# Transposed x and memory as inputs, the second weight unit in halves, and a new order of the first loads

## What is computed

```python
def hybrid_layer(x, mem, pos, g_mix, w_in, w_pa, w_pb, w_pm, w_o, g_mem, w_mkv, g_mlp, w_up, w_down):
    h = rms_norm(x, g_mix)
    z = h @ w_in                      # 1024 x 5632
    ...                               # three kinds of attention on parts of z, gates on the rest
    o_m = memory_attn(q_m * scale, rms_norm(mem, g_mem), w_mkv)
    ...
    x = x + y @ w_o
    hm = rms_norm(x, g_mlp)
    x = x + jnp.square(jax.nn.relu(hm @ w_up)) @ w_down
    return x
```

## Time and profile before

| | |
|---|---|
| median of three runs | 1577.0 us (1576.68 to 1578.81) |
| the profiled execution's own time | 1576.6 us |
| its span | 1574.8 us |
| TensorE busy | 1428.4 us, 91% of the span |
| VectorE, ScalarE, GpSimd busy | 578.9, 551.9, 673.6 us |
| share of TensorE and of DMA in the chain that ended last | 76% and 20% |
| moved by DMA | 395.40 MB, mean 251 GB/s |

### The profile page before, as it was taken

The page is one execution under the profiler, slowest core; times in us unless marked ns, Lnnn a source line. Parts: engine busy times, 40 slices in busy tenths (PEclk is TensorE's granted clock), DMA queues, the critical chain, the costliest instruction groups (busy, mean ns, idle before and its releaser), DMA issues.

```text
span 1574.8 us, 17946 instructions
## 1 busy us (share of the span) xinstructions
PE 1428.4 (91%) x7601; PEld 1015.6 (64%) x7601; DVE 578.9 (37%) x885; ACT 551.9 (35%) x709; POOL 673.6 (43%) x187
## 2 busy tenths in 40 slices
PE   8999999999999999999999999999996676666666
PEld 7877788877887778887799888978841121121111
DVE  4532423336262242334743886768510010010001
ACT  6356443433535545434343344574310000000001
POOL 5846588755784658786555775010000000000000
PEclk9999999999999999999999999999997788787788
DMA  8534457588553445659825444014999999999997
GB/s 296 188 112 157 149 173 240 182 304 315 174 182 126 146 147 183 226 181 337 320 87 183 147 145 154 14 68 142 419 407 427 427 429 427 427 428 428 428 427 292
DMA packets 115517, 395.40 MB, mean 251 GB/s; under 512 B 5719, under 2 KB 9620, under 8 KB 101996
## 3 DMA queue, kind: packets, MB, share of 16 engines
q1 hardware_dynamic: 113372, 388.70, 66.3%
q0 software_dynamic: 1520, 4.49, 0.8%
q10 hardware_dynamic: 544, 1.05, 0.2%
HBM read 393.16 MB, written 1.05 MB: 250 GB/s over the span
## 4 chain that ended last, share of the span: by engine, by line
PE 76%; DMA 20%; DVE 2%; ACT 1%; issue 1%; SPq 0%; DVEq 0%; ACTq 0%
PE psum L2284 18%; PE psum L2286 17%; PE psum L2285 17%; DMA ring<-in_w_e_down 7%; PE psum L1249 7%; DMA ring<-in_w_e_gate 6%; DMA ring<-in_w_e_up 6%; PE psum L1164 2%; PE psum L2437 1%; PE psum L2464 1%; PE psum L1025 1%; PE psum L2328 1%; PE psum L2513 1%; PE psum L824 1%; PE psum L823 1%; PE psum L825 1%
## 5 line engine op out<-in xcount | busy, mean ns | idle before, releaser
L655 POOL TENSOR_TENSOR ring_lo<-ring,ring_hi 128x2048 fp32r<-128x2048 f32 x118 | 537.9, 4565 | 230.5 <-ACT ring_hi L635 230.3
L635 ACT ACTIVATE ring_hi<-ring 128x2048 fp32r<-128x2048 f32 (+1 forms) x127 | 239.9, 1889 | 317.4 <-DMA ring<-in_w_down 108.5
L2286 PE MATMUL psum<-ring_hi,hT_hi 128*128 128x512 f32 (+2 forms) x848 | 327.7, 386 | 0.0
L2285 PE MATMUL psum<-ring_lo,hT_hi 128*128 128x512 f32 (+2 forms) x848 | 327.0, 386 | 0.0
L2284 PE MATMUL psum<-ring_hi,hT_lo 128*128 128x512 f32 (+2 forms) x816 | 323.0, 396 | 0.6 <-DVE ring_lo L2638 0.2
L1249 PE MATMUL psum<-arena 128*32 128x512 f32 x796 | 142.9, 706 | 64.2 <-DMA arena<-in_w_e_down 23.4
L1249 PE MATMUL psum<-ring,arena 128*32 128x512 f32 x720 | 132.8, 727 | 60.2 <-DMA ring<-in_w_e_gate 23.0
L2286 PEld LDWEIGHTS psum<-ring_hi,hT_hi 128*128 128x128 f32 x848 | 159.2, 188 | 32.4
L2285 PEld LDWEIGHTS psum<-ring_lo,hT_hi 128*128 128x128 f32 x848 | 159.5, 188 | 28.6
L2284 PEld LDWEIGHTS psum<-ring_hi,hT_lo 128*128 128x128 f32 x816 | 153.3, 188 | 37.6 <-issue 6.8
L1249 PEld LDWEIGHTS psum<-arena 128*32 128x32 f32 x796 | 32.2, 127 | 164.9 <-issue 73.6
(11 more groups left out here) (467 smaller groups left out, 1930.3 us busy)
## 6 DMA issues: line engine op xcount, KB each, us to landing
ring<-in_w_in SPq DMA_DIRECT2D x59, 1024.0 KB, 5.1
ring<-in_w_up SPq DMA_DIRECT2D x32, 1024.0 KB, 5.5
ring<-in_w_down SPq DMA_DIRECT2D x32, 1024.0 KB, 5.3
ring<-in_w_e_down SPq DMA_DIRECT2D x16, 2048.0 KB, 20.4
arena<-in_w_e_up SPq DMA_DIRECT2D x14, 2048.0 KB, 20.6
arena<-in_w_e_down SPq DMA_DIRECT2D x12, 2048.0 KB, 23.5
ring<-in_w_e_gate SPq DMA_DIRECT2D x12, 2048.0 KB, 22.7
arena<-in_w_e_gate SPq DMA_DIRECT2D x12, 2048.0 KB, 22.9
```

What stands on the lines that cost most here:

```text
L635: act.activation(slot_hi(u)[:, 0:c, :], slot(u)[:, 0:c, :], ACT.Copy).then_inc(hi_sb, 1)
L655: eng.tensor_tensor(slot_lo(u)[:, 0:c, :], slot(u)[:, 0:c, :], slot_hi(u)[:, 0:c, :].bitcast(F32), ALU.subtract).then_inc(done, 1)
L2285: pe.matmul(dst, hi(k0 + k), w_lo, start=False, stop=False)
L2286: last = pe.matmul(dst, hi(k0 + k), w_hi, start=False, stop=stop and k == nk - 1)
```

## The change

The host passes x and the memory transposed as well (`x_t`, `mem_t`, both 1024 x 256) and the gains of `norm_mix` as 128 x 16 (`gain_cols`).

- **x in layer 0.** ScalarE and SyncE load `x_t` in halves into the place of `xn`; `hT_hi` and `hT_lo` are made from there, chunk by chunk alternately with the pieces of unit 0. The sixteen transposes of x in layer 0 and that of the gain rows go. The plain x is loaded later: ScalarE waits for unit 2 and issues it, and squares it after the high parts of units 2 and 3.
- **Unit 1 in halves.** Its load, high part, low part and products come in two halves. VectorE makes the low part of unit 2 too.
- **Memory.** The transposes of both layers go. In layer 0 GpSimd issues the load of the memory after the low part of unit 3 (and a wait for x), that of `mem_t` after unit 4's, that of the rest of `consts` after unit 5's (and a wait for the memory). In layer 1 SyncE loads `mem_t` after unit 3. ScalarE copies `mem_t` to psum, where VectorE reads it as before. The memory's row factor is computed in layer 0 alone, with a square root of its own.
- **The rest.** `keep_busy` runs five matmuls, not four. Semaphore counts follow.

```diff
-LO_VECTOR = [(l, u) for l in range(DEPTH) for u in SPLIT if (l == 0 and u < 2) or (u >= 50 and u % 4 == 2)]
+LO_VECTOR = [(l, u) for l in range(DEPTH) for u in SPLIT if (l == 0 and u < 3) or (u >= 50 and u % 4 == 2)]
...
             sp.sem_inc(slots_free, R1)
+            sp.dma_start(cols[:, 0:16], w["gain_cols"]).then_inc(const_in, 16)
             sp.dma_start(consts[:, 0:P], w["consts"][:, 0:P]).then_inc(const_in, 16)
-            gain_rows(0, "norm_mix", const_in)
...
+                    if l == 0 and u == 1:
+                        for half in range(2):
+                            cs = slice(2 * half, 2 * half + 2)
+                            sp.dma_start(slot(1)[:, cs, :], src[:, cs, :]).then_inc(landed(1) if half else half_in, 16)
+                        sp.dma_start(xT[:, 4:8, :], x_src[:, 4:8, :]).then_inc(rest_in, 16)
+                        continue
                     load(u, src, l * UNITS1 + u + 1)
+                    if l and u == R1 - 1:
+                        sp.dma_start(memT, w["mem_t"].rearrange("(c p) t -> p c t", p=P)).then_inc(late_in, 16)
...
             pe.wait_ge(const_in, 32)
-            pe.transpose(psum[:, 7, 0:16], rows1[0:16, :], ident[0:16, 0:16]).then_inc(cols_full, 1)
-            pe.wait_ge(x_in, 16)
-            half_to_features(x, 0)
-            keep_busy(6, 4)
+            keep_busy(6, 5)
             first_unit()
-            pe.wait_ge(rest_in, 16)
-            half_to_features(x, 1)
+            second_unit()
...
-                if l == 0:
-                    pe.wait_ge(cols_sb, 2)
-                pe.wait_ge(mem_in, 32)
-                to_features(mem_tok)
...
-            x_src = w["x"].rearrange("b (t p) d -> p (b t) d", p=P)
-            act.dma_start(x[:, :, 0:UN], x_src[:, :, 0:UN]).then_inc(x_in, 16)
-            act.dma_start(x[:, :, UN:D], x_src[:, :, UN:D]).then_inc(rest_in, 16)
+            act.dma_start(xT[:, 0:4, :], w["x_t"].rearrange("(c p) t -> p c t", p=P)[:, 0:4, :]).then_inc(x_in, 16)
...
+            high_half(1, g_feat[:, 0, 0, :], 0, xT)
+            act.wait_ge(slot_in[2], 16)
+            act.dma_start(x[:, :, :], w["x"].rearrange("b (t p) d -> p (b t) d", p=P)).then_inc(x_in, 16)
...
+                if l == 0:
+                    high_parts(5, 5)
+                    act.wait_ge(mem_in, 16)
+                    for t in range(TT):
+                        act.activation(mem_sq[:, t, :], mem_tok[:, t, :], ACT.Square, accum_out=means[:, TT + t:TT + t + 1]).then_inc(sq_a, 1)
+                    high_parts(6, 6)
...
+                    act.wait_ge(rows_in, 16)
+                else:
+                    act.wait_ge(late_in, 16 * (N_LATE + l))
+                act.wait_ge(turn_lo, l * 18 + 8)
+                for half in range(2):
+                    act.activation(flat[2 + half].rearrange("p (k t) -> p k t", k=4), memT[:, 4 * half:4 * half + 4, :], ACT.Copy)\
+                       .then_inc(mem_f, 1)
+                high_parts(7 if l == 0 else 4, 14)
...
-            pool.wait_ge(rest_in, 16)
-            pool.wait_ge(slot_in[2], 16)
-            pool.dma_start(mem_tok, w["mem"].rearrange("b (t p) d -> p (b t) d", p=P)).then_inc(mem_in, 16)
-            pool.dma_start(consts[:, P:], w["consts"][:, P:]).then_inc(mem_in, 16)
...
                     split_lo(pool, l, u)
+                    if l == 0 and u == 3:
+                        pool.wait_ge(x_in, 32)
+                        pool.dma_start(mem_tok, w["mem"].rearrange("b (t p) d -> p (b t) d", p=P)).then_inc(mem_in, 16)
+                    if l == 0 and u == 4:
+                        pool.dma_start(memT, w["mem_t"].rearrange("(c p) t -> p c t", p=P)).then_inc(rows_in, 16)
+                    if l == 0 and u == 5:
+                        pool.wait_ge(mem_in, 16)
+                        pool.dma_start(consts[:, P:], w["consts"][:, P:]).then_inc(mem_in, 16)
```

More of the change, by code:

```diff
@@ L2345, in first_unit, with second_unit @@
                 last.then_inc(slots_free, 1)
+            def second_unit():
+                for half in range(2):
+                    pe.wait_ge(lo_v, UC + half + 1)
+                    for t in range(TT):
+                        last = split_product(DB[1][:, t, :], tokens(hT_hi, t), tokens(hT_lo, t), 2 * half, 1, nk=2, first=2 * half,
+                                             start=half == 0, stop=False)
+                last.then_inc(slots_free, 1)
             def late_rows():
@@ L2571, in _, with low_half @@
         def _(dve):
-            def low_half(half, gain, ready):
+            def low_half(half, gain, ready, features=None):
                 for k in range(4):
@@ L2576, in low_half @@
                         dve.wait_ge(turn_a, ready + k + 2)
-                    dve.scalar_tensor_tensor(out=hT_lo[:, 4 * half + k, :], in0=flat[2 + half][:, k * T:(k + 1) * T],
+                    src = flat[2 + half][:, k * T:(k + 1) * T] if features is None else features[:, 4 * half + k, :]
+                    dve.scalar_tensor_tensor(out=hT_lo[:, 4 * half + k, :], in0=src,
                                              scalar=gain[:, 4 * half + k:4 * half + k + 1],
@@ L2638, in low_piece @@
                 dve.tensor_tensor(slot_lo(0)[:, k, :], slot(0)[:, k, :], slot_hi(0)[:, k, :].bitcast(F32), ALU.subtract).then_inc(lo_v, 1)
-            dve.wait_ge(cols_full, 1)
-            dve.tensor_copy(cols[:, 0:16], psum[:, 7, 0:16]).then_inc(cols_sb, 1)
-            dve.wait_ge(cols_sb, 1)
-            low_piece(0)
-            low_half(0, g_feat[:, 0, 0, :], 0)
-            for k in range(1, UC):
+            dve.wait_ge(const_in, 32)
+            for k in range(UC):
+                dve.wait_ge(turn_a, k + 1)
+                dve.scalar_tensor_tensor(out=hT_lo[:, k, :], in0=xT[:, k, :], scalar=g_feat[:, 0, 0, k:k + 1],
+                                         in1=hT_hi[:, k, :].bitcast(F32), op0=ALU.mult, op1=ALU.subtract).then_inc(turn_lo, 1)
@@ L2646, in _ @@
                 low_piece(k)
-            split_lo(dve, 0, 1)
+            for half in range(2):
+                cs = slice(2 * half, 2 * half + 2)
+                dve.wait_ge(hi_sb, UC + half + 1)
+                dve.tensor_tensor(slot_lo(1)[:, cs, :], slot(1)[:, cs, :], slot_hi(1)[:, cs, :].bitcast(F32), ALU.subtract).then_inc(lo_v, 1)
             for l in range(DEPTH):
-                low_half(1, g_feat[:, 0, l, :], l * 18 + 4)
+                low_half(1, g_feat[:, 0, l, :], l * 18 + 4, None if l else xT)
@@ L2659, in _ @@
-                dve.tensor_scalar(means, means, 1.0 / D, EPS, ALU.mult, ALU.add).then_inc(r_v, 1)
-                dve.wait_ge(sq_a, l * 11 + 7)
-                dve.reciprocal(r_all, roots).then_inc(r_v, 1)
-                dve.wait_ge(r_v, l * 7 + 3)
+                    dve.wait_ge(cols_sb, 1)
+                cs = slice(0, TT)
+                dve.wait_ge(sq_a, l * 12 + 4)
+                dve.tensor_reduce(means[:, cs], sums, AX_X, ALU.add).then_inc(r_v, 1)
+                dve.wait_ge(r_v, l * 9 + 1)
@@ L2680, in _ @@
                 z_tile(1)
+                if l == 0:
+                    cm = slice(TT, 2 * TT)
+                    dve.wait_ge(sq_a, 7)
+                    dve.tensor_scalar(means[:, cm], means[:, cm], 1.0 / D, EPS, ALU.mult, ALU.add).then_inc(r_v, 1)
+                    dve.wait_ge(sq_a, 8)
+                    dve.reciprocal(r_mem, roots[:, cm]).then_inc(r_v, 1)
+                    dve.wait_ge(r_v, 6)
                 for half in range(2):
-                    dve.wait_ge(turn_full, l * 8 + 3 + half)
+                    dve.wait_ge(mem_f, 2 * l + half + 1)
                     for k in range(4):
@@ L2910, in high_piece @@
                 act.activation(slot_hi(0)[:, k, :], slot(0)[:, k, :], ACT.Copy).then_inc(hi_sb, 1)
-            high_piece(0)
-            act.wait_ge(cols_sb, 1)
-            high_half(0, g_feat[:, 0, 0, :], 1)
-            for k in range(1, UC):
+            act.wait_ge(const_in, 32)
+            act.wait_ge(x_in, 16)
+            for k in range(UC):
+                act.activation(hT_hi[:, k, :], xT[:, k, :], ACT.Copy, scale=g_feat[:, 0, 0, k:k + 1]).then_inc(turn_a, 1)
                 high_piece(k)
+            for half in range(2):
+                cs = slice(2 * half, 2 * half + 2)
+                act.wait_ge(slot_in[1] if half else half_in, 16)
+                act.activation(slot_hi(1)[:, cs, :], slot(1)[:, cs, :], ACT.Copy).then_inc(hi_sb, 1)
+            high_half(1, g_feat[:, 0, 0, :], 0, xT)
+            act.wait_ge(slot_in[2], 16)
+            act.dma_start(x[:, :, :], w["x"].rearrange("b (t p) d -> p (b t) d", p=P)).then_inc(x_in, 16)
             for l in range(DEPTH):
```

112 lines of the change are left out of this document (65 added, 47 removed).

## The result

The changed kernel takes 1588.55 us in the median of five runs (1587.6 to 1589.82), the kernel before in the same comparison 1577.32: a ratio of 1.007 with a 95% interval of 1.0059 to 1.0082. It is slower by 11 us. The forecast was 1571.4, faster; the time is outside its range, and beyond the rival that gave 1580.5.

A forecast was written before the change was run, and what follows sets the result against it. TensorE was taken to set the pace to about 1100 us, expert loads after. 1.3 + 1.2 + 1.75 + 1.75 - 0.4 = 5.6 us off 1576.6 gave 1571.0, as a median 1571.4; range 1568.8 to 1575.0.

The forecast's parts named there:

- the rival that gave 1580.5: Layer 0, plain x landing very late, at 31 us: GpSimd and ScalarE wait, kernel slower at 1580.5 us; chance 0.04.
- What bounds the kernel: TensorE sets the pace to about 1100 us, expert loads after; a microsecond saved on TensorE early is one of the total.
- Step 1: Start of the kernel: unit 0 begins at 7.55 and ends at 13.85 us, a gain of 1.3 us, ends +2.3 and -0.3.
- the rival in which it is up already: Start: the clock is already up when unit 0 starts, 0.8 us are not lost, 1570.6 us; chance 0.12.
- Step 2: Layer 0, second half of x's transposes gone and the slower matmul after it: a gain of 1.2 us.
- Step 3: Memory's transposes gone in layers 0 and 1: a gain of 1.75 us in each.
- Step 4: Layer 0, units 2 to 7 in the new order of loads: nearly every unit ready when TensorE wants it, 0.4 us lost.
- ends 0 and 3: Layer 0, units 2 to 7: the least and most us that waits under the new order were taken to cost.
- all landings at 11.3: Case behind the loss of 3 us: loads take the longest row, the memory costing 2.1 us and mem_t 2.5, not added.
- the slower rival: Layer 0, plain x lands very late and holds GpSimd and ScalarE; slower by over 0.2% from a landing at 30.7; chance 0.04.
- Unit 4 ... ready at 30.1; wanted 30.5: Layer 0: x lands at 21.1, then squares 2.5, high part 1.92, low part 4.6 us make unit 4 ready at 30.1.
- ready at L + 9.0: Layer 0: if x lands at L, unit 4 is ready at L + 9.0 and TensorE waits L + 9.0 - 30.5.

The follow-up runs named there:

- e8: e5 with the loads of memory, mem_t and tables issued by SyncE and the tables' transposes behind unit 2; 1576.2 us, against 1578.4 before the change.
- e5: The changed kernel with half_r made by ScalarE, silu_c moved before the MLP and the memory's mean written to psum; 1576.66 us, against 1578.4 before the change.
- e10: e9 with the mean of x written to psum instead of SBUF in layer 0; 1574.98 us, against 1578.38 before the change.
- e9: e8 with ScalarE's unit 4 high part before x's sums, the square-root table loaded early and silu_c's tanh later; 1574.66 us, against 1578.7 before the change.
- e6: e5 with x issued at once, not behind unit 2's landing, and the tables' transposes behind unit 2; 1580.07 us, against 1578.4 before the change.

## Why the prediction was wrong, step by step

**What bounds the kernel: right.** TensorE's shift at L1039, 11.46 us (1060.15 against 1048.69), is the shift of the end, 11.2 in the medians. That they agree so closely is in part luck, as the stretch behind L1039 differs by up to 3 us between profiles.

**Step 1, the start: right, a little better.** The constants landed at 4.97 (forecast 5.4) and unit 0 began at 7.13 (7.55). The gain columns, in rows of 64 B, landed 3.1 us after issue and the constants, in rows of 512 B, 3.7, so the rule of 512 B for line rate (the Trainium skill, DMA: Bandwidth & Descriptors, the table at its head) decided nothing here. The clock did take its share, with matmuls 0.57 and 0.43 us apart, to 8.5 in this execution; the rival in which it is up already did not come about.

**Step 2, x's transposes: right.** Unit 1 ended at 18.69 (18.46 and 0.23), forecast 19.3; before, its last matmul began at 21.57.

**Step 3, the memory's transposes: right.** In layer 1 the stretch from x's second transposes to the first wait block is 486.00 - 425.23 = 60.77 us; before it was 475.02 - 412.49 = 62.53:

```profile
412.49 0.71 PE L2328 MATMUL psum<-consts,x 128*128 128x128 f32 x5
```

That is 1.76 us gained, forecast 1.75.

**Step 4, the new order: this failed,** as its term of 0.4 us lost (ends 0 and 3) came out at 17.6: the first wait block of layer 0 stands 12.7 us later, although 3.1 were gained up to the end of unit 1 and some 1.75 on the memory's transposes. Even its end of 3 was too small by its own rows: "all landings at 11.3" left out the load of x, for which the slower rival gives 4.4.
- "Unit 4 ... ready at 30.1; wanted 30.5" followed the loads, ScalarE and GpSimd, and never VectorE. TensorE needs two things for unit 4, its low part and free psum banks, and the banks wait for VectorE's row factor and z tiles. The low part was done at 34.0; the bank that unit 4 needs came free at 45.95. The step costed `half_r`, silu_c and the means at nothing without naming them. In the trace before the first two cost next to nothing (0.17 and 0.30), since they happened to fall into the 2.7 us in which GpSimd was idle; the mean had its wait already, 0.64 us.
- The unseen wait is 2.77 and 10.41 us on VectorE, 12.46 before unit 4, and 1.6 more behind it for the clock (0.50 granted from 46 to 48 us).
- The tables were costed as 0.35 us of transposes, without their landing. They stood in SyncE's queue behind unit 3 and landed at about 20.4: 1.64 us of waiting, and eight slow matmuls behind it, some 1.5 us (0.51 granted from 22 to 24 us). Unit 2's own low part, "ready at 19.3", ended at 20.28, so the tables alone are not to blame for the wait; in e8, without them, TensorE still waits 0.61 us for it. That is why unit 3 ended at 33.4 and not at 30.5.
- x landed at 24.9, not 21.1. By the forecast's own formula (ready at L + 9.0) that gives 33.9, and the low part ended at 34.0. In the changed kernel this is hidden behind VectorE's wait, in e5 and e8 it is the 2.2 us that remain. The slower rival had this mechanism and the right relation, but L was well under the 30.7 it needs; what made the kernel slower was none of the rivals.

The terms sum up: 33.38 instead of 30.5, 12.6 of waiting and 1.6 of slow clock put the first wait block of layer 0 at 91.21, 12.7 later than before. Layer 1's 1.76 make it 10.98 at 475 us. With these waits removed, the profile of e10 stands 5.45 us earlier than that of before at this place, 4.9 at L1039 and 4.2 in its own time (1572.36 against 1576.6): most of the 5.6 us forecast were there to be had in that execution, with an order of loads and of ScalarE's work that the change did not have. What the runs show is less, the 3 us of e9's ratio.

## What to carry to other kernels

Before a step is moved, ask for every small operation that it carries along what the neighbouring engine was doing when its short duration was measured; a duration of 0.17 us from a gap is no price for a place without one. Where GpSimd works nearly without pause, keep VectorE's scalings from SBUF to SBUF and its operations with two SBUF inputs, however small, off every path that TensorE waits for: write them to psum, give them to ScalarE, or put them where nobody waits. Look in the trace before for one shape with two durations: 0.61 and 5.04 us stood there next to each other. And an engine kept busier by a change isn't only later itself: it shuts out the other one (e6).
